# Expert weights in two wide spans, all of w1 before w3, instead of four narrow spans with w1 and w3 in turn

## The reference

```
logits = h @ w_r
vals, idx = top_k(logits, 2);  wts = softmax(vals)
comb = sum(one_hot(idx, 8) * wts)
out = 0
for e in range(8):
    out += comb[:, e:e+1] * ((silu(h @ w1e[e]) * (h @ w3e[e])) @ w2e[e])
x = x + gt2 * rmsnorm(out)
```

## Time and profile before

| | |
|---|---|
| time, median of 3 runs | 1732.68 us (1731.38 to 1733.14) |
| the profiled execution's own time | 1733.21 us |
| its span | 1731.4 us |
| TensorE busy | 1629.6 us (94%) |
| VectorE busy | 957.6 us (55%) |
| ScalarE busy | 537.4 us (31%) |
| SyncE's DMA queue | 474.25 MB, 71.6% of 16 engines' span |

### The profile page before, as it was taken

The page is one execution under the profiler, slowest core; times in us unless marked ns, Lnnn a source line. Parts: engine busy times, 40 slices in busy tenths (PEclk is TensorE's granted clock), DMA queues, the critical chain, the costliest instruction groups (busy, mean ns, idle before and its releaser), DMA issues.

```text
span 1731.4 us, 21272 instructions
## 1 busy us (share of the span) xinstructions
PE 1629.6 (94%) x8420; PEld 1116.9 (65%) x8420; DVE 957.6 (55%) x1356; ACT 537.4 (31%) x685; POOL 4.0 (0%) x13
## 2 busy tenths in 40 slices
PE   6999999999999999998999999999989999878886
PEld 4688675888888885797788734887348863323322
DVE  6688765544446776698698713986129851110102
ACT  5421334300000006414577402773127730000001
POOL 0000000000000000000000000000000000000000
PEclk9999999999999999999999999999999999999998
DMA  9420976223321325317799999999999999999996
GB/s 339 160 98 1 332 255 227 71 96 96 96 97 38 131 94 201 135 62 292 298 355 374 335 408 407 412 409 410 415 406 412 410 409 411 408 412 410 409 414 262
DMA packets 164826, 476.25 MB, mean 275 GB/s; under 512 B 10114, under 2 KB 41316, under 8 KB 150372
## 3 DMA queue, kind: packets, MB, share of 16 engines
q1 hardware_dynamic: 162896, 474.25, 71.6%
q10 hardware_dynamic: 1812, 0.41, 0.1%
HBM read 473.58 MB, written 1.05 MB: 274 GB/s over the span
## 4 chain that ended last, share of the span: by engine, by line
PE 71%; SPq 14%; DVE 5%; issue 3%; ACT 3%; DMA 3%; ACTq 1%; DVEq 0%; POOL 0%; POOLq 0%
SPq L796 11%; PE ps L929 10%; PE ps L931 10%; PE ps L930 10%; PE ps L1389 7%; PE ps L1381 6%; PE ps L1383 6%; PE ps L1289 6%; SPq L800 3%; PE ps L893 2%; PE ps L1329 2%; PE ps L852 2%; DMA ring<-in_e_w 1%; DMA work<-in_e_w 1%; PE ps L1260 1%
## 5 line engine op out<-in xcount | busy, mean ns | idle before, releaser
L1289 PE MATMUL ps<-ring,work 128*64 128x512 f32 x960 | 224.5, 616 | 38.5 <-DMA ring<-in_e_w 35.8
L2575 DVE TENSOR_TENSOR norms<-work,ps 64x256 f32<-64x256 f32 x70 | 29.7, 424 | 330.7 <-ACT work L1851 329.2
L929 PE MATMUL ps<-ring_rounded 128*128 128x512 f32 (+1 forms) x536 | 190.5, 355 | 2.9 <-DVE norms L2357 1.6
L1289 PEld LDWEIGHTS ps<-ring,work 128*64 128x64 f32 x960 | 72.7, 141 | 177.6 <-issue 176.3
L1987 DVE TENSOR_TENSOR ring_rounded<-ring,hT_rounded 128x2048 fp32r<-128x2048 f32 x72 | 163.0, 2286 | 17.2 <-ACT hT_rounded L1874 17.2
L931 PE MATMUL ps<-ring_rounded 128*128 128x512 f32 (+1 forms) x472 | 163.3, 346 | 0.0
L1874 ACT CAST hT_rounded<-ring 128x2048 fp32r<-128x2048 f32 x72 | 136.8, 1916 | 33.7 <-PE ps L1383 18.8
L931 PE MATMUL ps<-mixT_rounded,ring_rounded 128*128 128x512 f32 x328 | 127.6, 389 | 0.0
L929 PE MATMUL ps<-mixT_rounded,work_rounded 128*128 128x512 f32 x304 | 118.3, 389 | 0.0
L930 PE MATMUL ps<-hT_rounded,work_rounded 128*128 128x512 f32 x304 | 118.3, 389 | 0.0
L929 PEld LDWEIGHTS ps<-ring_rounded 128*128 128x128 f32 x536 | 101.3, 189 | 19.3 <-issue 2.3
(11 more groups left out here) (312 smaller groups left out, 2855.6 us busy)
## 6 DMA issues: line engine op xcount, KB each, us to landing
ring<-in_e_w SPq DMA_DIRECT2D x288, 1024.0 KB, 18.3
ring<-in_w_mod SPq DMA_DIRECT2D x20, 2048.0 KB, 10.2
mixT<-in_e_w SPq DMA_DIRECT2D x24, 1024.0 KB, 18.6
work<-in_e_w SPq DMA_DIRECT2D x24, 1024.0 KB, 18.5
ring<-in_w_in SPq DMA_DIRECT2D x11, 2048.0 KB, 8.0
ring<-in_w SPq DMA_DIRECT2D x22, 1024.0 KB, 8.0
ring<-in_w_mod SPq DMA_DIRECT2D x8, 1024.0 KB, 11.6
ring<-in_w_out SPq DMA_DIRECT2D x4, 2048.0 KB, 15.5
```

The source lines that it names most:

```text
L929: pe.matmul(acc, w_high_, x_high_, start=first, stop=False)
L1289: ins = pe.matmul(narrow_bank(b)[H * w:H * w + H, :], xsel[:, k, 0:H], piece_words(e, pair[w])[:, at_:at_ + BLK], start=(k == 0), stop=(k ...
```

## The change

The spans become [0,1,2,3] and [4,5,6]. A piece of w1 or w3 is now one row tile (128 rows) with all columns of the span: 2048 columns (1 MiB, rows of 8 KB) in the first span, 1536 columns (0.75 MiB, rows of 6 KB, in a slot of 1 MiB) in the second. All eight w1 pieces of a span come first (`"g"`), then the eight of w3 (`"u"`). An expert has 46 pieces: 16 of 1 MiB, 16 of 0.75 MiB, and the 14 of w2 as before. The order is g0, u0, g1, w2 of blocks 0 and 1, u1, w2 of blocks 2 to 6.

In mid a piece of the second span has 9 matmuls and split operations of 1536 columns. The four Silus of the first span stand together behind its last w1 piece, and its four products behind its last w3 piece; in the second span Silus of blocks 4 and 5 follow the last w1 piece, that of block 6 follows a piece in the middle of w3, and the three products follow the last w3 piece. Silu and product of a block share one of four buffers. In few a Silu covers two blocks (gate of one block on partitions 0 to 63, of the next on 64 to 127) and so does a product, so there are 4 of each instead of 7 Silus and 14 products; the work is waited for piece by piece.

```diff
-SPANS = [[b for b in (2 * s, 2 * s + 1) if b < NB] for s in range((NB + 1) // 2)]
+SPANS = [[0, 1, 2, 3], [4, 5, 6]]
-ROUNDS = [2 * KD // (4 // len(blocks)) for blocks in SPANS]
 def gate_up(s):
-    return [("gu", s, i) for i in range(ROUNDS[s])]
+    return [(w, s, k) for w in "gu" for k in range(KD)]
-ORDER = sum([gate_up(s) + (downs(s - 1) if s else []) for s in range(NS)], []) + downs(NS - 1)
+ORDER = gates(0) + ups(0) + gates(1) + downs(0, 1) + ups(1) + downs(2, 3, 4, 5, 6)
+gates_at = {("g", 0, KD - 1): (0, 1, 2, 3), ("g", 1, KD - 1): (4, 5), ("u", 1, KD // 2): (6,)}
+hidden_at = {("u", 0, KD - 1): (0, 1, 2, 3), ("u", 1, KD - 1): (4, 5, 6)}
+turns_at = {("g", 1, KD // 2 - 1): (0, 1), ("u", 1, KD // 2 - 1): (2, 3), ("dn", 2, 1): (4,), ("dn", 3, 1): (5,),
+            ("dn", 4, 1): (6,)}
...
+        def hidden_words(b):
+            return esg[:, b % 4, :] if b % 4 < 2 else hid[:, b % 4 - 2, :]
         def gate_bank(b):
-            return ps[2 + b % 2]
+            return ps[(2, 3, 6, 4, 2, 3, 4)[b]]
         def up_bank(b):
-            return ps[3] if len(SPANS[b // 2]) == 1 else ps[6 + b] if b < 2 else ps[4 + b % 2]
+            return ps[(7, 5, 0, 1, 5, 2, 3)[b]]
...
@@ sync @@
-                    if kind == "gu":
-                        tiles = 4 // len(SPANS[n])
-                        width = PIECE // tiles
-                        w = e_w3 if i % 2 else e_w1
-                        src = expert_rows(w, expert, (i // 2) * tiles * P, tiles, 2 * BLK * n, width)
-                        sp.dma_start(dst.rearrange("p (k n) -> p k n", k=tiles), src).then_inc(piece_in[s], 16)
+                    if kind in "gu":
+                        width = BLK * len(SPANS[n])
+                        w = e_w3 if kind == "u" else e_w1
+                        src = expert_rows(w, expert, i * P, 1, BLK * SPANS[n][0], width)
+                        sp.dma_start(dst[:, 0:width].rearrange("p (k n) -> p k n", k=1), src).then_inc(piece_in[s], 16)
...
@@ tensor, mid @@
+                hidden("g", 0, 0)
+                pe.wait_ge(xsel_low_ready, e + 1)
+                hidden("g", 0, 1)
+                pe.wait_ge(swt_done, e + 1)
+                hidden("u", 0, 0)
+                hidden("u", 0, 1)
+                pe.wait_ge(esg_ready, e * STEPS + 2 * len(SPANS[0]))
+                hidden("g", 1, 0)
+                turn(0)
+                turn(1)
+                hidden("g", 1, 1)
+                pe.wait_ge(hid_ready, e * STEPS + 2 * len(SPANS[0]))
+                down(0)
+                down(1)
+                pe.wait_ge(esg_ready, e * STEPS + 2 * (NB - 1))
+                hidden("u", 1, 0)
+                turn(2)
+                turn(3)
+                hidden("u", 1, 1)
+                down(2)
+                turn(4)
+                pe.wait_ge(esg_ready, e * STEPS + STEPS)
                 next_gather(e)
...
@@ scalar, mid (vector likewise, with hidden_at for the products) @@
-                    if used in gates_end:
-                        for b in SPANS[used[1]]:
-                            gate(b)
+                    for b in gates_at.get(used, ()):
+                        gate(b)
```

More of the change, by code:

```diff
@@ L1271, in every_second, with few_hidden @@
                 return a.rearrange("p (i c q) -> p i q c", i=2, q=2)[:, j // 2, j % 2]
-            def few_hidden(e, s, part_):
+            def few_hidden(e, w, s, part_):
                 H = FEW
[L1275 to L1295, removed]
@@ L1370, in mid, with piece_product @@
                 pe.sem_inc(extra_ready, 3)
-                def piece_product(key, outs, high, low, first, last, parts=(range(4),)):
+                def piece_product(key, outs, high, low, first, last, parts=None):
+                    parts = parts or (range(len(outs)),)
                     n = e * PER + PLACE[key]
@@ L1394, in piece_product, with hidden @@
                     return ins
-                def hidden(s, part_):
+                def hidden(w, s, part_):
                     blocks = SPANS[s]
                     nb = len(blocks)
[L1399 to L1412, removed]
+                    outs = [(up_bank if w == "u" else gate_bank)(b)[:] for b in blocks]
+                    for k in range(part_ * (KD // 2), (part_ + 1) * (KD // 2)):
+                        ins = piece_product((w, s, k), outs, [xsel_high[:, k, :]] * nb, [xsel_low[:, k, :]] * nb,
+                                            nb if k == 0 else 0, nb if k == KD - 1 else 0)
+                    if part_:
+                        ins.then_inc(gu_ready if w == "u" else egate_ready, 2 * nb)
                 def turn(b):
@@ L1541, in big @@
-                    if s:
-                        down(s - 1)
-                    turn(s)
-                down(NS - 1)
+                    for k in range(KD):
+                        key = (w, s, k)
+                        wait_piece(pe, e, key)
+                        for q in range(nb):
+                            ins = pe.matmul(ps[2 + q][:], (xsel2 if t else xsel)[:, k, :],
+                                            piece_words(e, key)[:, q * BLK:(q + 1) * BLK],
+                                            start=(k == 0), stop=(k == KD - 1))
+                        if t == 1:
+                            frees(ins, e, key)
@@ new lines, in hidden, with gate_and_up @@
+                    ins.then_inc(gu_ready if w == "u" else egate_ready, nb)
+                def gate_and_up(s, between=lambda: None):
+                    first, nb = e * STEPS + 2 * SPANS[s][0], len(SPANS[s])
+                    if s:
+                        pe.wait_ge(hid_ready, first)
+                    hidden("g", s, 0)
+                    pe.wait_ge(esg_ready, first + nb)
+                    hidden("g", s, 1)
+                    pe.wait_ge(esg_ready, first + 2 * nb)
+                    between()
+                    hidden("u", s, 0)
+                    pe.wait_ge(hid_ready, first + nb)
+                    hidden("u", s, 1)
@@ L2620, in mid @@
                     used = ORDER[n - 2] if n >= 2 else None
-                    if used in ups_end:
-                        for b in SPANS[used[1]]:
-                            gate(b)
-                    if used == ("gu", 1, 5) and e + 1 < NE:
+                    for b in hidden_at.get(used, ()):
+                        gate(b)
+                    if used == ("g", 1, 5) and e + 1 < NE:
                         select(e + 1)
-                    if used in turns_at:
-                        for b in turns_at[used]:
-                            turned(b)
+                    for b in turns_at.get(used, ()):
+                        turned(b)
                 if e + 1 < NE:
@@ L2647, in big, with add @@
                 dve.tensor_copy(swt2, ps[7][:, 0:SEQ]).then_inc(extra_done, 1)
-                def add(s):
-                    for b in SPANS[s]:
+                def add(*blocks):
+                    for b in blocks:
                         for t in range(2):
```

325 lines of the change are left out of this document (181 added, 144 removed).

## The result

The changed kernel takes 1723.1 us (median, 1722.2 to 1724.4, 4 runs) against 1732.9 us, a ratio of 0.9944 with the 95% interval 0.9929 to 0.9960. That is 9.8 us less (6.9 to 12.3). The forecast was 12.9 us less, 1719.8, with a range of 1714 to 1730. A second set gave 0.9948 (0.9935 to 0.9962). The profiled execution took 1724.4 us with a span of 1722.6, 8.8 us under that of before.

The account below looks back on a forecast made before the run. TensorE bounds e0, the DMA the stage from 1008 us. Six experts save 13.0 us, the rest of e1 1.2, the ring costs 1.3, other parts 0: 12.9 us less, 1719.8 us by the median, range 1714 to 1730.

Parts of the forecast that it names:

- The bound: Expert part: e0 in mid is bound by TensorE, the stage from 1008 to 1716 us by the DMA.
- Part 1, the rates: w1 and w3 transfers: longer rows make each expert 2.17 us shorter, 105.3 instead of 107.4 us.
- Rivals B and C: Weight transfers: 6 KB rows move in two parts (1727, chance 0.09); w1 and w3 keep 4 KB-row rates (1730, chance 0.08).
- The straight line through three sizes: DMA price by the row, from 2, 4 and 8 KB rows: 0.53 ns plus 4.75 ns for each 2 KB.
- The 0.5 MiB of the ring: Full ring at the start of the DMA stage: 0.5 MiB less has landed, costing 1.3 us.
- Part 2: Weight transfers: 46 instead of 42 for each expert cost 0 us, as seven in flight hide their fixed cost.
- Part 3, the clusters: e0 in mid: grouped Silus and products pass with 0.5 to 1 us to spare; 0 us, bounds -2 and +5.
- the 0.55 us that I gave VectorE: Mid, behind g0's last piece: VectorE's low part is ready at T + 6.7 us and needed at T + 7.25.
- Part 4: Few-experts and the end: fewer Silus and products stand off the path, 0 us; tail stays 14.8 us, give or take 2.
- do the experts keep up: DMA stage: experts stay no slower than their weights, the ring filling in mid stages and draining in few stages.
- the margin of 3.8 MiB: Ring at the end of e2: 10.2 MiB lie ready or nearly, of 14 it holds; called thin.
- rival D: Mid stages: clusters break the split's lead; beyond about 3 us each counts three times, 1743 at 10 us; chance 0.10.

Follow-up runs that it names:

- after_rows: Changed kernel with each w1 and w3 piece made of two half rows (4 and 3 KB rows, wrong weights), as many transfers: 1736.0 us, 1.0014 of the kernel before.
- after_cols: Changed kernel with each piece fetched by two transfers, w1 and w3 by column halves, w2 by partition halves: 2030.6 us, ratio 1.1725 to the kernel before.
- after_turns: Changed kernel with hidden blocks transposed three times, 6.7 us more TensorE work in each mid stage: 1.0040 of the kernel before, 16.7 us over the changed kernel.
- after_again: The changed kernel run once more, unaltered, as base for other runs: 1725.1 us, ratio 0.9948 to the kernel before.
- after_bytes: Changed kernel with the ring filled by bytes, a 0.75 MiB piece taking 0.75 MiB instead of a 1 MiB slot: 1724.1 us, 0.9942 of the kernel before.
- after_13: Changed kernel with 13 ring slots instead of 14: ratio 0.9975 to the kernel before, 5.4 us more than the changed kernel.

## Why the prediction was right, and where it was not

**The bound.** Right. e0 is bound by TensorE and the rest by the DMA; every experiment that left the transfers fast moved the way that says, if not always by the amount.

**Part 1, the rates.** Right to 0.7%: 8 KB rows 420 GB/s (419.4 forecast), 6 KB rows 416 to 418 (415), an expert 105.3 and 105.5 us (105.3). Rivals B and C are out by these windows, and `after_rows` shows that the rows carry the gain. The straight line through three sizes was enough to price a size that the trace didn't have.

**The 0.5 MiB of the ring.** The mechanism was right and the size too small: 1.2 MiB behind at 1016 us, 3.1 us instead of 1.3. I had counted 18 pieces of e1, two of them small: the 14 of the full ring and four more. But slots still set the pace behind that: e1 gives ten free between 993 and 1014 us. In the kernel before these are 10 MiB, 508 GB/s and more than the DMA moves. Here eight of the ten take a small piece, 8 MiB or 406 GB/s, and that holds the DMA back (315 against 405 GB/s from 1000 to 1016). The slots of 1 MiB filled with 0.75 during e0's first span count for little, since its second span gives most of it back.

**Part 2.** Right: no cost of more transfers (`after_cols`' w1 and w3 windows). The section of the Trainium skill from which the prediction takes its 2 us (DMA: Bandwidth & Descriptors, Anatomy of one DMA) gives them for transfers issued from GpSimd. Here SyncE issues them.

**Part 3, the clusters.** Nearly right. e0 ends 1.15 us later, 0.85 of it before the first piece. The seven Silus of e2 are four of 596 ns and three of 610 ns, close to the 597 ns of before. The chain of waits shows that the four Silus are now on it, with the high part and the low part behind them:

```profile
893.69 0.49 ACT norms L1949
894.17 1.80 ACT hT_rounded L1943
896.00 2.30 DVE ring_rounded L2061
898.35 1.19 PE ps L1419 x4
```

So the 0.55 us that I gave VectorE were spent to the end, but TensorE stands for only 0.2 us more over e0 (0.6 behind VectorE at L1419, 0.4 before).

**Part 4 and "do the experts keep up".** This is the step that failed. I had e1 unchanged and the margin of 3.8 MiB as enough. e1 ended 5.6 us later by its own doing, 4.6 of them the gap at the branch to mid and the lower clock behind it, and behind e2 3.4 us of DMA time were gone. At 2.5 us for a MiB 5.6 us are 2.2 MiB of the margin. That the one caused the other is argued from this and from `after_turns`, not shown by a run without the gap alone. I had the mechanism as rival D, but its cause as broken clusters within mid. The margin doesn't ask where TensorE loses its time.

**The sum.** Forecast 12.9. Less 1.8 (ring), 3.4 (behind e2) and 0.8 (the end took 15.6 us from the last piece's matmuls instead of 14.8) is 6.9. The profiled executions differ by 8.8 and the medians by 9.8. The 2 to 3 us that are left over lie within the rounding of the rates over 690 us; these runs don't place them. So the total came out nearer to the forecast than its parts did, and that is luck.

What stays open is why TensorE waits 4 to 5 us at some branches in one build and 1 to 2 in another. It comes again in the same place for the same kernel (4.71 us in `after_again`, e1) and elsewhere in others (4.94 us at the end of e3 in `after_turns`, 4.33 us at the end of e4 in `after_bytes`). The traces give a lead. In each of these four gaps a packet of 16 KB moves on the queue that the profile calls `q8 instruction`. It starts 1.6 to 2.3 us after the end of TensorE's last matmul, and TensorE goes on 1.5 to 1.6 us after its end. In `after_rows` and `after_13` the packet starts about 1 us before that last matmul ends, TensorE goes on 1.5 us after its end too, and the gap is 1.75 and 1.37 us. In the kernel before, with 1.66 us, it moves only behind the gap. So the long gaps look like waits for code that arrives late, which isn't shown. No experiment here changed the layout of the code alone or the time of this packet, and what sets it stays open.

## What to carry to other kernels

Where the DMA engines are the bound, fit a price by the row to the windows that you have, and lengthen the rows: from 4 to 8 KB it was 2.7% of the rate here, and the order of the computation may well be bent to it. Then look at what a ring holds in bytes when its slots are counted in pieces, and at the stage in which compute still is the bound: the gain of faster transfers ends where the ring is full. When two stages take turns as the bound, work out the margin between them in bytes and ask of every engine's delay ahead of it, not only of those that you change.

## What the runs showed of the hardware

- A row of a transfer has a price of its own: the line 0.53 ns + 4.75 ns for each 2 KB (all 16 engines together) fits 2 KB (388 GB/s), 4 KB (408) and 8 KB (419), and held at 3 KB (402) and 6 KB (416 to 418).
- Two transfers of 64 partitions in place of one of 128 cut the rate to 54 to 61%: 226 to 255 GB/s for 8 KB rows, against 419. The whole kernel went from 1723 to 2144 us or more. Two transfers of half the columns cost nothing but the shorter rows (408 and 402 GB/s for 4 and 3 KB rows, as in `after_rows` with one transfer).
- TensorE stood 4.3 to 4.9 us in "issue" where it branches between two versions of the code, at places that differ from build to build (four traces), and went on 1.5 to 1.6 us after the end of a 16 KB packet of the queue `q8 instruction`.
- Behind such a gap the granted clock was at the lower level: 0.54 over L1280 in the changed kernel, which took 3.64 us instead of 1.99; 0.71 over the 32 matmuls in `after_bytes`, 9.92 us instead of 7.09.
- Where the ring is full, the rate is slots given free times bytes in a slot: with ten slots in 21 us the DMA ran at 315 GB/s for 16 us when they took 8 MiB, and at 405 when they took 10.
